# A hybrid retention/HGRN2 step: three small loads moved to ScalarE's queue, x loaded first and in six pieces

## What is computed

```
mod = silu(c) @ w_ada + b_ada                  # once for c, once for c_ctx
shift, scale, gate = split(mod, 3)
h = rms_norm(x, norm_w)                        # mean of x*x over 2048 channels
h = h * (1 + scale) + shift
proj = h @ w_in                                # 2048 -> 9216, nine parts
...
out = concat(o_retention, o_hgrn) @ w_out
y = rms_norm(x + gate * out, final_norm_w)
```

## Time and profile before

| | us |
|---|---|
| median of three runs | 1432.33 (1431.62 to 1432.93) |
| the profiled execution's own time | 1431.45 |
| its span, first to last instruction | 1429.6 |
| TensorE busy | 1407.1 |
| VectorE busy | 965.4 |
| ScalarE busy | 495.6 |

### The profile page before, as it was taken

One profiled execution on the slowest core, in us unless ns is written; L12 is line 12 of the kernel. 1 busy time (PEld: TensorE's weight loads), 2 busy tenths in 40 slices (PEclk: granted clock), 3 DMA queues, 4 the chain that ended last, 5 costly groups with the idle time before them and its releaser, 6 DMA issues.

```text
span 1429.6 us, 25607 instructions
## 1 busy us (share of the span) xinstructions
PE 1407.1 (98%) x10235; PEld 1185.1 (83%) x10235; DVE 965.4 (68%) x1292; ACT 495.6 (35%) x893; POOL 365.6 (26%) x292
## 2 busy tenths in 40 slices
PE   7999999999999999999999999999999999999997
PEld 5778898889888988898889888988898888888886
DVE  4555676667888787878787878666676668632345
ACT  4323243334333433343334333423342334321234
POOL 0000114311432153215321532153115315301220
PEclk9999999999999999999999999999999999999999
DMA  9994222223332333233333333223223347183235
GB/s 379 410 418 156 78 89 87 87 84 126 126 119 96 126 126 119 97 125 126 119 103 118 126 119 110 67 86 88 93 67 97 89 148 257 46 289 108 89 104 205
DMA packets 68723, 196.62 MB, mean 138 GB/s; under 512 B 7809, under 2 KB 16273, under 8 KB 63633
## 3 DMA queue, kind: packets, MB, share of 16 engines
q1 hardware_dynamic: 68592, 195.15, 40.0%
q10 hardware_dynamic: 32, 0.02, 0.0%
HBM read 174.41 MB, written 16.53 MB: 134 GB/s over the span
## 4 chain that ended last, share of the span: by engine, by line
PE 94%; DMA 4%; DVE 1%; SPq 0%; issue 0%; ACT 0%; DVEq 0%; ACTq 0%
PE ps L1908 10%; PE ps L1910 10%; PE ps L1909 10%; PE ps L1756 8%; PE ps L1858 8%; PE ps L1758 8%; PE ps L1757 8%; PE ps L2088 5%; PE ps L2090 5%; PE ps L2089 5%; DMA area<-in_w_mod 4%; PE ps L1925 2%; PE ps L1763 2%; PE ps L1765 2%; PE ps L1764 2%; PE ps L1740 1%
## 5 line engine op out<-in xcount | busy, mean ns | idle before, releaser
L1097 DVE TENSOR_TENSOR w_lo<-area,w_hi 128x1024 fp32r<-128x1024 f32 x144 | 184.1, 1279 | 270.7 <-ACT w_hi L650 270.4
L650 ACT ACTIVATE w_hi<-area 128x1024 fp32r<-128x1024 f32 x144 | 152.6, 1060 | 492.9 <-PE ps L1910 272.3
L1908 PE MATMUL ps<-w_hi,hT_hi 128*128 128x512 f32 x640 | 252.5, 394 | 0.0
L1910 PE MATMUL ps<-w_hi,hT_lo 128*128 128x512 f32 x640 | 249.4, 390 | 0.0
L1909 PE MATMUL ps<-w_lo,hT_hi 128*128 128x512 f32 x640 | 249.2, 389 | 0.0
L1756 PE MATMUL ps<-hT_hi,w_hi 128*128 128x512 f32 x512 | 205.5, 401 | 1.8 <-DVE hT_lo L1150 1.8
L1758 PE MATMUL ps<-hT_hi,w_lo 128*128 128x512 f32 x512 | 199.7, 390 | 0.0
L1757 PE MATMUL ps<-hT_lo,w_hi 128*128 128x512 f32 x512 | 199.6, 390 | 0.0
L1908 PEld LDWEIGHTS ps<-w_hi,hT_hi 128*128 128x128 f32 x640 | 120.2, 188 | 25.8 <-issue 1.6
L1910 PEld LDWEIGHTS ps<-w_hi,hT_lo 128*128 128x128 f32 x640 | 120.1, 188 | 25.3
L1642 POOL TENSOR_TENSOR area<-area 128x320 f32<-128x320 f32 x56 | 55.6, 993 | 332.0 <-PE ps L1925 279.6
(11 more groups left out here) (263 smaller groups left out, 2455.2 us busy)
## 6 DMA issues: line engine op xcount, KB each, us to landing
area<-in_w_in SPq DMA_DIRECT2D x144, 512.0 KB, 3.6
area<-in_w_mod SPq DMA_DIRECT2D x32, 1024.0 KB, 9.1
area<-in_w_out SPq DMA_DIRECT2D x38, 512.0 KB, 3.7
gate_raw<-in_w_gate SPq DMA_DIRECT2D x32, 512.0 KB, 3.6
o_hi_scratch<-area SPq DMA_DIRECT2D x14, 320.0 KB, 2.2
o_lo_scratch<-area SPq DMA_DIRECT2D x14, 320.0 KB, 2.8
hT_hi<-o_hi_scratch SPq DMA_DIRECT2D x14, 320.0 KB, 7.1
hT_lo<-o_lo_scratch SPq DMA_DIRECT2D x14, 320.0 KB, 7.6
```

The costliest lines, as they stand in the source:

```text
L650: act.activation(w_hi[:, n % 2, :], raw[:, n % 3, :], ACT.Copy).then_inc(wt_hi.sem, 1)
L1097: v.tensor_tensor(w_lo[:, n % 2, :], raw[:, n % 3, :], w_hi[:, n % 2, :].bitcast(F32), ALU.subtract).then_inc(wt_lo.sem, 1)
L1908: mm(out, hT_hi[:, k, tile_cols(t)], w_hi[:, n % 2, w], start=k == 0, stop=False)
L1910: i = mm(out, hT_lo[:, k, tile_cols(t)], w_hi[:, n % 2, w], start=False, stop=k == KT - 1)
```

## The change

The three small loads leave SyncE's queue and become the first instructions of ScalarE, ahead of its table load. SyncE's first instruction is now the first load of x. x comes in six loads of 4, 4, 3, 2, 2 and 1 slices. TensorE sums slice 13 and VectorE slice 15, where it was the other way round.

```diff
-X_SPANS = ((0, 4), (4, 8), (8, 12), (12, 14), (14, 16))
+X_SPANS = ((0, 4), (4, 8), (8, 11), (11, 13), (13, 15), (15, 16))
...
-PE_SQUARES = (1, 3, 5, 7, 9, 11, 15)
-DVE_SQUARES = (0, 2, 4, 6, 8, 10, 12, 13, 14)
+PE_SQUARES = (1, 3, 5, 7, 9, 11, 13)
+DVE_SQUARES = (0, 2, 4, 6, 8, 10, 12, 14, 15)
...
-            sp.dma_start(c_raw[:, 0, :], c_ctx.rearrange("(p k) -> p k", k=KT)).then_inc(c_in.sem, 16)
-            sp.dma_start(c_raw[:, 1, :], c[0].rearrange("(p k) -> p k", k=KT)).then_inc(c_in.sem, 16)
-            sp.dma_start(con[:, 0:NSTART], consts[:, 0:NSTART]).then_inc(con_start.sem, 16)
             for j in range(X_LOADS):
                 ks = slice(*X_SPANS[j])
                 sp.dma_start(x_in[:, ks, :], x_columns[:, ks, :]).then_inc(x_landed[j].sem, 16)
...
         @block.scalar
         def _(act):
+            act.dma_start(c_raw[:, 0, :], c_ctx.rearrange("(p k) -> p k", k=KT)).then_inc(c_in.sem, 16)
+            act.dma_start(c_raw[:, 1, :], c[0].rearrange("(p k) -> p k", k=KT)).then_inc(c_in.sem, 16)
+            act.dma_start(con[:, 0:NSTART], consts[:, 0:NSTART]).then_inc(con_start.sem, 16)
             act.preload_act_table_set("natural_log_exp_and_others")
```

## The result

The changed kernel takes 1438.80 us (median of six runs, 1437.36 to 1440.22); the kernel before, measured beside it, 1432.14 (six runs). The ratio is 1.0045, interval 1.0035 to 1.0055: 6.7 us slower. The profiled execution has a span of 1437.2 against 1429.6. The prediction had 1431.4 and a range up to 1435.7.

The account below looks back on a forecast made before the run. TensorE was taken to bound the whole, the stream of loads the opening. Issues 0, six loads 0, swap 0 and stream -0.9 us from the runs' median of 1432.33 gave 1431.4 us, range 1430.4 to 1435.7.

Parts of the forecast that it names:

- What bounds the kernel: Whole kernel: TensorE bounds it except in the opening; a shift it has at 112 us is carried to the end unchanged.
- x first: Opening: x issued 1.38 us earlier moves the stream of loads forward by 0.5 to 1.38 us, taken as 0.9.
- Issues moved to ScalarE: Before ScalarE's table load: three issues take 1.33 to 2.25 us, the table load ends at 3.4 to 4.3; cost 0.
- The cover: Opening: small loads land early enough, the constants near 5 us, that TensorE's time in hand keeps the 0.9 us gain.
- my limits: Opening: latest landings that keep the gain, c until 6.3 us and the constants until 7.6.
- my first rival: Opening: each small load waits for a whole load of x, constants land at 12.1; +3.6 us, 1435.9; chance 0.17.
- my terms: Chain of x sums: idle products on TensorE take 4.65 us after the constants land, then eight pairs of sums 10.1.
- The price of that rival: Full late landing: sum complete at 26.9, 5.0 us late, less 0.3 and 1.07 in hand, gives +3.6 us.
- My last sign of being wrong: TensorE after the opening: no more waits for w_mod at 64 and 110 us would show the forecast wrong.
- The time in hand: TensorE could be late at 30.4 us by 0.3 us, and by 1.07 more from later waits on w_mod.
- Six loads and the swap: Opening: x in six loads and slices 13 and 15 exchanged change the time by 0.

Follow-up runs that it names:

- e8: Changed kernel with c_ctx and c merged into the constants, one load at the head of SyncE's queue: 1429.69 us, ratio 0.9986 to the kernel before.
- e7: Changed kernel with c_ctx back at the head of SyncE's queue, c and the constants still on ScalarE's: 1432.68 us, ratio 1.0004 to the kernel before.
- e4: Changed kernel with the first load of x cut into four loads of one slice: 1433.23 us, ratio 1.0007 to the kernel before.
- e9: Changed kernel, constants first on SyncE's queue, exponential behind the second square, silu(c) awaited only before the first w_mod chunk: 1430.57 us, ratio 0.9993 to before.
- e6: Changed kernel with a fifth slot for w_mod: 1435.79 us, ratio 1.0032 to the kernel before.
- e1: Changed kernel with the three small loads back at the head of SyncE's queue: 1432.02 us, ratio 0.9996 to the kernel before.
- e11: e8 with the five loads of x and the split of slices of the kernel before: 1429.91 us, ratio 0.9986 to the kernel before.

## Why the prediction was wrong

**What bounds the kernel: right in outline.** The steady part carried the shift unchanged (1307.6 us before, 1307.8 after), and the opening decided everything.

**x first, 0.9 us of the stream: right as far as it went.** The first chunk of w_mod landed at 20.16 instead of 21.24, 1.1 us earlier, and e8 shows the gain reaching the end.

**Issues moved to ScalarE: right.** 0.43 to 0.45 us each, table load done at 3.45; nothing waited for it.

**The cover: the step that failed.** I took the landings of loads that run alone, 2.1 and 2.3 us, for loads beside x. They took 8.6 and 10.9, so that c came at 9.8 and the constants at 12.6, where my limits were 6.3 and 7.6. This was my first rival, and I gave it 0.17 against 0.48. Its landing was worked out as 12.1 us and came at 12.6, with whole loads taking turns, where in fact single packets do; here both come to nearly the same. The rule of the Trainium skill that stood beside it ("DMA: Bandwidth & Descriptors", section "Queues, rings and completion order", round robin by packet) held for the profile's packets: the counts of 90 and 91 are one for one. The same section has an engine drain a packet of some 9 to 17 descriptors before it turns to the other queue; the counts do not bear that out, for each turn was a single row of 64 or 10,240 B, and the counts decide. I had treated turns as one of several possibilities, though no row spoke against them.

The limits themselves were about 1 us too generous. e7 had its constants at 7.5, inside the limit, and the gain was not to be seen: the sum was complete at 23.55, where my terms give 7.6 + 4.65 + 10.05 = 22.3. The two terms that were too small there are the same as in the next paragraph.

**The price of that rival: too small, 3.6 instead of 6.7 us.** The time of the sum and the time made up behind it were mis-sized. The sum was complete 7.1 us late, not 5.0: constants 0.5 later, idle products 5.25 us (12.69 to 17.94) instead of 4.65, and 11.1 us of sums instead of eight pairs in 10.05. The idle products took anything from 4.2 (e4) to 5.3 us (e8, e9) in the profiles, at a granted clock shown as 1.00; what decides it is open. The sums were longer by a wait of 1.07 us for the last addition of VectorE, which had to wait for the last square. That is put down to the ring of four buffers by argument from the rows; no run has a deeper ring: ScalarE had made five squares and then stood still for 5.86 us until TensorE had read square 1, so that the eleven others, 7.00 us, came behind the wait instead of ahead of it. (e8, whose ring did not stop, has the same wait of 1.07 us, because its squares kept only just ahead of the sums; so the wait by itself is no mark of the ring.) And of the 1.07 us that TensorE was to make up later, it made up none, since the four slots tied the stream to TensorE: the late first use of a chunk held back the fifth load. e6 isolates this at 2.6 us by the medians, 2.95 by the profiles. My last sign of being wrong, no more waits for w_mod, failed for the same reason: the stream was late together with TensorE, which still waited 0.54 us for the last chunk. The time in hand itself was also read from the wrong row: PE's waits add up to 1.07 us, PEld's to 2.2, and with that one the sums close.

**Six loads and the swap worth nothing: right** (e1, e11).

## What to carry to other kernels

In these runs a small load on a second queue beside large packets landed only after as many large packets as it had of its own, not after 2 us. What the first instructions wait for belongs ahead of the large loads, merged into one load if its issues are too many; only what is needed late may go to the second queue. The queue counts in a short window show such turns directly. And ask of a late chain not only who waits for it, but whose buffers it holds: a full stream with few slots goes dry behind it, and the catching up that the waits seem to promise goes with it.

## What the runs showed beside

The granted clock fell in four profiles (e1, e4, e9 and e11) and not in the others, each time at the same wait of 1.75 us in which TensorE stands still for VectorE (in e11 within it, in e1 at its end, in e4 and e9 up to half a microsecond behind it). Eight other profiles, that of before among them, have this wait of 1.75 us and no fall. In e9 by windows:

```profile
44.00:45.00 1.00, 0.34 (x14) 1.00 1.01 410
45.00:46.00 1.00, 0.00 (x0) 1.00 0.92 369
46.00:47.00 1.00, 0.91 (x3) 0.66 1.05 430
47.00:48.00 1.00, 1.00 (x4) 0.50 1.06 438
48.00:49.00 1.00, 1.00 (x3) 0.50 1.03 426
49.00:50.00 1.00, 1.00 (x4) 0.63 1.01 418
```

0.50 is 1.2 GHz, and a product there takes 0.63 us instead of 0.40:

```profile
46.09 0.56 PE L1755 MATMUL ps<-hT_hi,w_hi 128*128 128x512 f32 x1 [1.75 <-DVE hT_lo L1150]
46.45 0.63 PE L1756 MATMUL ps<-hT_lo,w_hi 128*128 128x512 f32 x1
...
50.05 0.40 PE L1756 MATMUL ps<-hT_lo,w_hi 128*128 128x512 f32 x1
```

The missing shares add up to 0.34 + 0.50 + 0.50 + 0.37 = 1.7 us, as they do in the other three, and by about so much the steady part came later than the sum above gives: 1.5 us in e1, 1.8 in e4, 1.6 in e9 and in e11. A fall that comes in one execution and not in the next is part of the scatter between runs of one kernel, and larger than the gain that the change was after. The mean granted clock of each execution points the same way: of the 25 executions of the kernel before that e1 is compared with, 14 had 0.998 and a span of 1429.5 to 1430.0 us, nine had 0.997 and 1430.0 to 1431.2, two had 0.996 and 1431.9 to 1432.2.
